# Two-layer hybrid decoder step: where the second expert choice of a half runs, and which engine adds expert rows that run alone

## The chip, the cores and the metric

The kernel is one launch on one NeuronCore of a Trainium2 chip. The metric is device time in microseconds (us) of one execution, input tensors and outputs in HBM. TensorE does matrix products, VectorE elementwise work, reductions and top-8 searches, ScalarE activations and copies, GpSimd issues the gathers, SyncE issues all other DMAs.

## The reference, cut to what matters

Two layers run over a prompt of 512 tokens (four tiles of 128) and over 8 sample tokens with caches. In each layer a token gets three mixers (a dilated window attention, a gated delta rule, a stick-breaking attention) and then PEER, a choice of 16 of 16384 one-neuron experts by each of 8 heads:

```python
s1, i1 = lax.top_k(s[:, :, 0], PEER_TOPK)
s2, i2 = lax.top_k(s[:, :, 1], PEER_TOPK)
top_s, pick = lax.top_k(cand_s, PEER_TOPK)            # 16 x 16 sums per head
act = jax.nn.gelu(jnp.einsum('nd,ned->ne', xk, u_tab[ik]))
return jnp.einsum('ne,ned->nd', gk * act, v_tab[ik])
```

So every token fetches 128 rows of 1024 floats from `peer_u`, takes a dot with each, and adds up 128 rows of `peer_v` with weights. The modulation vectors `silu(c) @ w_ada + b_ada` (6144 columns a layer) are needed by every normalisation.

## The kernel before, in words

The prompt is cut into halves of two tiles, and a half of one layer is a unit; there are four (layer 0 tiles 0, 1; layer 0 tiles 2, 3; layer 1 the same). The program is a row of windows, each an `nc.Block()` that all engines enter and leave together (`window`, line 2503). The first computes a part of layer 0's modulation. The second runs the mixers of unit 0 beside the mixers of the sample, with the modulation of layer 1 in it (`late`, line 2566). Then come four windows `k` = 0 to 3, each with the experts of unit `k` beside the mixers of unit `k + 1`; the last has the sample's second layer beside the experts of unit 3. In the profile the second window ends at 992 us, and the four expert windows begin at 993, 1937, 2785 and 3644 us.

The mixers of a unit are a list of stages (`token_mixers`, line 2276): normalise, `project` (14.7 MB of weights), unit lengths, heads, two attentions, delta rule in three stages, gated norm, `out_projection` (4 MB), normalise again, `queries` (4 MB), `choose_tile` for tile 0, `choose_tile` for tile 1. Each stage is a Python generator per engine, cut into ticks, and ends with a barrier (`stage_over`) of the lane's engines. `choose_tile` (line 1753) is VectorE work: `choose` (line 294) finds the 16 best by MAX8, FIND_INDEX8 and MATCH_REPLACE8 in 14 pieces; the last tick raises `chosen`.

The experts of a unit are a list of phases: all rows of `u` of tile a; rows of `v` of a and of `u` of b in turn; all rows of `v` of b. In what follows these are the `u` stretch (128 rows), the mixed stretch (256) and the `v` stretch (128, called alone, since its phase has one batch). A row is one gather of 128 partitions x 4 KB (512 KB) by GpSimd into one of GR = 12 buffers (line 2392); it waits for the buffer's last reader. A `u` row is one VectorE instruction (line 2442). A `v` row is either a product on TensorE with a diagonal matrix that ScalarE makes (lines 2479 and 2496; four matmul records of 512 columns) or one scalar_tensor_tensor on VectorE into ACC (line 2458). `on_dve` (line 168) gives VectorE every fourth row from row 8 on, 30 of 128. GpSimd waits for `chosen` before row 0 of each `u` batch.

What sets the order is a plan made ahead: every stage has a length (`paced`), `when` spreads the stages' ticks over 0 to 1 by these lengths, the expert rows are spread evenly over the same 0 to 1, and `merge` emits each engine's instructions in that one order. Nothing else than the order ties mixers to rows; each engine then runs its own stream in order. The lengths sum to 554 where the next unit has tiles 0, 1 (window k = 1) and to 606 where it has tiles 2, 3 (k = 0 and 2), each choice being 59 of it.

`modulate` (line 593) streams `w_ada` through a ring of SBUF tiles. SyncE's program for one tick: wait until a tile is used (613), load the next (614), wait for VectorE's result (618), store it (619), wait until the store has landed (620), load the next bias (621). Layer 1 is done in two stages of six tiles of 512 columns (2 MB) with a ring of two, one beside each choice of unit 0 (`meanwhile`).

SC[0] and SC[1] hold the scores of the two tiles. TMP, scratch of `project`'s convolution (lines 415 and 416), lies on SC[1].

## Time and profile before, and how to read it

| | us |
|---|---|
| median of 3 runs | 4719.75 (4712.13 to 4724.38) |
| the profiled execution, its own time | 4694.12 |
| its span, first to last instruction | 4692.3 |
| TensorE busy | 3425.7 (73%) |
| VectorE busy | 2843.8 (61%) |
| GpSimd busy | 2587.5 (55%) |
| mean granted TensorE clock | 0.843 |

A view of stretches gives, for each stretch of the span (us from its start), the busy time and instruction count of each engine, the granted clock as a share of full speed, the mean busy share of the 16 DMA engines, and GB/s. A view of waits gives the waiting engine, tile and line, what released it, then us in total, times, longest. A timeline row gives start, duration, engine, line, operation, count, and in brackets the idle time before it. A group row gives count, busy us, mean ns, and idle time before it with the releasers.

### The profile page before, as it was taken

To read this page: it belongs to the slowest core of one execution; us is meant where nothing else is said; L and a number is where in the kernel's file an instruction comes from. 1 tells how busy PE (TensorE), PEld (TensorE's weight loads), DVE (VectorE), ACT (ScalarE), POOL (GpSimd) and SP (SyncE) were. 2 spreads that over 40 slices of the span, in tenths; PEclk is the share of its full clock that TensorE was granted. 3 is DMA by queue.
4 is the path that set the end of the run, shared out by engine and by line. 5 is a ranking of instruction groups with operands and counts; after the bars stand their busy time and mean duration, and the time that the engine had idled before them with its cause. 6 is when DMAs were issued, how large, how long until landed. Compare 5 with 4: busy or idle time off the path is not lost. (4 is left out here: it accounts for less than half of the span.)

```text
span 4692.3 us, 42307 instructions
## 1 busy us (share of the span) xinstructions
PE 3425.7 (73%) x11982; PEld 1910.2 (41%) x11982; DVE 2843.8 (61%) x5777; ACT 877.2 (19%) x2045; POOL 2587.5 (55%) x2244
## 2 busy tenths in 40 slices
PE   5966768539298889575887967498898436748897
PEld 2624543126154554262455426255553113213351
DVE  1225552556866648787774688868649767584322
ACT  1113110011142112112321211242221011000120
POOL 0000362025767757687774667777656767665563
PEclk8986789759589999796998988799999767869896
DMA  6451375549989989899998889999988989999995
GB/s 229 139 180 56 101 227 177 187 104 320 354 318 345 385 308 339 331 399 342 366 376 320 306 334 395 353 346 361 367 306 308 378 303 348 362 382 377 336 330 154
DMA packets 586674, 1401.71 MB, mean 299 GB/s; under 512 B 67314, under 2 KB 287659, under 8 KB 585244
## 3 DMA queue, kind: packets, MB, share of 16 engines
q0 software_dynamic: 306176, 1107.44, 63.6%
q1 hardware_dynamic: 261836, 274.77, 17.7%
q10 hardware_dynamic: 18432, 16.79, 1.1%
q8 instruction: 101, 1.65, 0.1%
q14 instruction: 129, 1.06, 0.1%
HBM read 1387.11 MB, written 11.88 MB: 298 GB/s over the span
## 5 line engine op out<-in xcount | busy, mean ns | idle before, releaser
L2496 PE MATMUL bank<-arena 128*128 128x512 f32 (+1 forms) x3264 | 1589.6, 636 | 200.5 <-PEq L2493 117.9
L2392 POOL DMA_INDIRECT arena<-in_peer_u_dram,arena x1056 | 1279.6, 1212 | 693.2 <-issue 303.1
L2392 POOL DMA_INDIRECT arena<-in_peer_v_dram,arena x1056 | 1160.5, 1099 | 749.2 <-PE bank L2496 448.4
L2442 DVE CUSTOM_DVE_ANT_0 arena<-arena 128x1024 f32<-128x1024 f32 (+1 forms) x1056 | 1269.8, 1224 | 447.5 <-DMA arena<-in_peer_u_dram,arena 417.4
L2496 PEld LDWEIGHTS bank<-arena 128*128 128x128 f32 (+1 forms) x3264 | 614.8, 196 | 1013.6 <-issue 869.5
L2479 ACT ACTIVATE arena<-arena 128x128 f32<-128x128 f32 (+1 forms) x816 | 301.5, 394 | 1072.9 <-PE bank L2496 686.1
L2458 DVE SCALAR_TENSOR_TENSOR arena<-arena 128x1024 f32<-128x1024 f32 x232 | 297.6, 1283 | 243.6 <-DMA arena<-in_peer_v_dram,arena 223.3
L799 PE MATMUL bank<-arena 128*128 128x256 f32 (+3 forms) x1472 | 368.9, 414 | 101.0 <-PEq L792 95.9
L2138 POOL DMA_INDIRECT arena<-in_cache_sb_k_dram,arena x64 | 84.0, 1312 | 550.4 <-POOLq L2131 530.2
L799 PEld LDWEIGHTS bank<-arena 128*128 128x128 f32 (+1 forms) x1472 | 247.0, 170 | 220.8 <-issue 156.1
L641 PE MATMUL bank<-arena 128*9 128x512 f32 x384 | 180.3, 627 | 66.9 <-PEq L637 45.9
L796 PE MATMUL bank<-arena 128*128 128x256 f32 x768 | 177.7, 392 | 18.6 <-PEq L792 18.6
L1565 PE MATMUL bank<-arena 128*128 128x256 f32 (+1 forms) x640 | 154.0, 399 | 40.6 <-PEq L1563 39.0
L796 PEld LDWEIGHTS bank<-arena 128*128 128x128 f32 x768 | 149.1, 196 | 48.5 <-issue 27.7
L718 PE MATMUL bank<-arena 128*128 128x128 f32 (+1 forms) x160 | 31.5, 360 | 178.6 <-PEq L714 178.6
L1565 PEld LDWEIGHTS bank<-arena 128*128 128x128 f32 (+1 forms) x640 | 113.1, 178 | 87.9 <-issue 62.3
L655 DVE TENSOR_TENSOR arena<-bank,arena 9x512 f32<-9x512 f32 x24 | 16.3, 679 | 194.9 <-DVEq L654 194.9
L2167 PE MATMUL bank<-arena 128*4 128x256 f32 x512 | 118.2, 386 | 17.2 <-PEq L2116 15.7
L1647 PE MATMUL bank<-arena 128*128 128x256 f32 x512 | 117.7, 385 | 4.7 <-PEq L1643 3.7
L641 PEld LDWEIGHTS bank<-arena 128*9 128x9 f32 x384 | 35.0, 94 | 203.7 <-issue 203.1
L1647 PEld LDWEIGHTS bank<-arena 128*128 128x128 f32 x512 | 97.9, 193 | 30.2 <-issue 17.8
L718 PEld LDWEIGHTS bank<-arena 128*128 128x128 f32 (+1 forms) x160 | 26.3, 204 | 192.1 <-issue 192.0
(339 smaller groups left out, 3730.0 us busy)
## 6 DMA issues: line engine op xcount, KB each, us to landing
arena<-in_w_in_dram SPq DMA_DIRECT2D x78, 1024.0 KB, 13.2
arena<-in_w_ada_dram SPq DMA_DIRECT2D x24, 2048.0 KB, 8.4
arena<-in_w_out_dram SPq DMA_DIRECT2D x24, 1024.0 KB, 13.0
arena<-in_peer_wq_dram SPq DMA_DIRECT2D x24, 1024.0 KB, 15.0
arena<-in_peer_u_dram,arena POOLq DMA_INDIRECT x1056, 7.4
arena<-in_peer_v_dram,arena POOLq DMA_INDIRECT x1056, 6.2
arena<-in_cache_sb_k_dram SPq DMA_DIRECT2D x128, 128.0 KB
arena<-in_cache_sb_v_dram SPq DMA_DIRECT2D x128, 128.0 KB
```

What stands on the lines that cost most here:

```text
L641: last = pe_.matmul(ps[n % 2][0:R9, 0:width], CT[:, k, :], W[n % ring][:, k, :], start=(k == 0), stop=(k == KD - 1))
L796: last = pe_.matmul(ps[t % BANKS][:, 0:n_], m.W[c % ring][:, k, off:off + P], m.HT[:, k, 0:n_], start=(k == 0), stop=(k == KD - 1))
L799: last = pe_.matmul(ps[t % BANKS][0:r, 0:hi - lo], m.HT[:, k, i * P:i * P + r], m.W[c % ring][:, k, 0:hi - lo], start=(k == 0), stop=(k == ...
L1565: last = pe_.matmul(bank(g)[0:r, 0:CW_], m.OT[:, k, i * P:i * P + r], m.W[j % ring][:, k, 0:CW_], start=(k == 0), stop=(k == KD - 1))
L1647: last = pe_.matmul(ps[h % 3][:, 0:n_], m.W[h // 2 % ring][:, k, (h % 2) * P:(h % 2 + 1) * P], m.HT[:, k, 0:n_], start=(k == 0), stop=(k = ...
L2138: pool_.indirect_dma_start(m.HALF[h % 4][:, j, :], None, rows, bass.IndirectOffsetOnAxis(ap=m.IDP[:, at:at + 1], axis=0)).then_inc(paged[h ...
L2167: last = pe_.matmul(ps[b % 2][0:NH, 0:AW], weights[:, half * HP + j, :], m.HALF[n % 4][:, j, :], start=(half == 0 and j == 0), stop=(half ...
L2392: pool_.indirect_dma_start(G_[g % GR][0:b.parts, :], None, tables[0 if which == "u" else 1], bass.IndirectOffsetOnAxis(ap=b.index[:, n:n + ...
L2442: vec.tensor_tensor_reduce(row, row, b.h, 1.0, 0.0, ALU.mult, ALU.add, b.AV[0:b.parts, n:n + 1]).then_inc(freed_by_dve, 1)
L2458: i_ = vec.scalar_tensor_tensor(ACC, G_[g % GR], b.AV[:, n:n + 1], ACC, ALU.mult, ALU.add)
L2479: act_.activation(DG[order % NDG][0:b.parts, 0:b.rows], b.mark, ACT.Copy, scale=b.AV[0:b.parts, mine:mine + 1]).then_inc(diag_ready, 1)
L2496: last = pe_.matmul(ps[6 + i][0:b.rows, :], DG[owners[g][1] % NDG][0:b.parts, 0:b.rows], G_[g % GR][0:b.parts, i * GBLK:(i + 1) * GBLK], s ...
```

## The change

The second choice of a unit leaves the list of stages and becomes a thread of its own in the next window, spread over the first 0.22 of its plan, with a lane's set of semaphores of its own. The modulation of layer 1 becomes one stage of 24 tiles of 256 columns (1 MB) with a ring of four, beside unit 0's first choice, and that stage gets length 80. The sums of lengths become 495 and 547 (516 in the second window). Where a phase holds one batch, VectorE gets every second `v` row from row 8 on (60 of 128). TMP gets room of its own, since SC[1] is now in use during `project`.

```diff
+ON_DVE_ALONE = 2
-    return not b.sample and n >= FIRST_ON_DVE and n % ON_DVE == ON_DVE - 1
+    return not b.sample and n >= FIRST_ON_DVE and n % b.every == b.every - 1
...
-            m.CWR = AR.room(P)[0:KW * CC, :]
             m.SMALL = AR.room(16)
-            scratch = SC[1].rearrange("p a b -> p (a b)")
-            m.TMP = [scratch[:, i * n_:(i + 1) * n_] for i in range(3)]
+            m.TMP = [AR.room(n_) for _ in range(3)]
+            m.CWR = m.TMP[2][0:KW * CC, 0:P]
...
-                        paced(choose_tile(u, e, 0, meanwhile[0:1]), 59), paced(choose_tile(u, e, 1, meanwhile[1:2]), 59)]
+                        paced(choose_tile(u, e, 0, meanwhile), 80 if meanwhile else 59)]
...
+            for phase in phases:
+                for which, b in phase:
+                    if which == "v":
+                        b.every = ON_DVE_ALONE if len(phase) == 1 else ON_DVE
...
+        def second_choice(u, span):
+            ticks, programs = LC.choose_tile(u, None, 1)
+            return [span[0] + (span[1] - span[0]) * (n + 1) / ticks for n in range(ticks)], programs
...
+            times += [(t, 3, "choice") for t in choice[0]]
...
-                      experts=programs.get(name, nothing)())
+                      experts=programs.get(name, nothing)(), choice=choice[1].get(name, no_choice)())
...
-        LP, LS = lane("prompt", ps[0:6]), lane("sample", ps[6:8])
+        LP, LS, LC = lane("prompt", ps[0:6]), lane("sample", ps[6:8]), lane("second_choice", [])
...
-        tiles = [AR.room(KD, GBLK) for _ in range(2)]
-        late = [LP.modulate(1, tiles, GBLK, half * MOD // 2, (half + 1) * MOD // 2) for half in range(2)]
+        late = [LP.modulate(1, [AR.room(KD, GBLK // 2) for _ in range(4)], GBLK // 2)]
...
+            choice = second_choice(u, (0.0, 0.22))
             if k < 3:
-                window(LP.token_mixers(units[k + 1]), [], phases)
+                window(LP.token_mixers(units[k + 1]), [], phases, choice=choice)
...
-                window([], LS.token_mixers(samples[1], (LAST_at, arena_cols)), phases + [[("u", s)], [("v", s)]], (0.0, 0.85))
+                window([], LS.token_mixers(samples[1], (LAST_at, arena_cols)), phases + [[("u", s)], [("v", s)]], (0.0, 0.85), choice)
```

## Rows read from the trace of the kernel before

**Rows 1.** Stretches: columns PE, PEld, DVE, ACT, POOL busy, PE clock, DMA share, GB/s.

```profile
1067.00:1296.00 229.00, 124.26 (x481) 89.49 (x479) 181.43 (x321) 28.63 (x82) 160.32 (x128) 0.75 0.94 343
...
1937.00:2146.00 209.00, 117.94 (x481) 97.49 (x481) 167.34 (x293) 27.10 (x71) 168.94 (x128) 0.76 1.00 385
2146.00:2562.00 416.00, 319.80 (x1234) 195.24 (x1234) 285.85 (x494) 109.34 (x257) 284.21 (x257) 0.88 0.95 356
2562.00:2785.00 223.00, 204.72 (x565) 97.12 (x563) 159.34 (x508) 47.15 (x118) 139.45 (x129) 0.99 0.86 309
2785.00:3000.00 215.00, 119.72 (x482) 98.70 (x482) 177.76 (x312) 30.98 (x78) 165.56 (x128) 0.75 1.01 388
...
3402.00:3644.00 242.00, 215.11 (x602) 107.21 (x600) 158.83 (x508) 48.76 (x122) 135.77 (x129) 0.96 0.83 298
3644.00:3882.00 238.00, 95.97 (x338) 45.30 (x338) 152.44 (x268) 20.11 (x42) 170.99 (x128) 0.65 0.92 348
...
4365.00:4590.00 225.00, 203.59 (x619) 97.37 (x620) 61.31 (x97) 47.51 (x120) 128.45 (x128) 0.95 0.92 336
```

**Rows 2.** Stretches inside the `v` stretch of window 1: `queries`, first choice.

```profile
2562.00:2618.00 56.00, 55.44 (x232) 35.10 (x231) 12.30 (x14) 15.22 (x38) 27.67 (x27) 1.00 0.80 274
2618.00:2700.00 82.00, 77.43 (x179) 32.99 (x177) 71.68 (x245) 17.87 (x45) 57.75 (x53) 1.00 0.92 328
```

**Rows 3.** Timelines: ScalarE's last score copy of unit 0, VectorE's last instruction of that window.

```profile
747.67 2.05 ACT L1683 COPY arena<-bank 128x512 f32<-128x512 f32 x4 [3.48 <-ACTq L1680]
...
991.47 0.17 DVE L373 TENSOR_TENSOR arena<-arena 64x16 f32<-64x16 f32 x1
```

**Rows 4.** Timeline of SyncE's queue, 756 to 946 us: tiles of `w_ada`, last stores.

```profile
756.22 1.02 SPq L614 DMA_DIRECT2D arena<-in_w_ada_dram  x2
...
775.32 0.39 SPq L614 DMA_DIRECT2D arena<-in_w_ada_dram  x1
...
910.12 0.39 SPq L614 DMA_DIRECT2D arena<-in_w_ada_dram  x1
...
918.89 0.39 SPq L614 DMA_DIRECT2D arena<-in_w_ada_dram  x1
...
937.34 9.12 SPq L628 DMA_DIRECT2D modulation<-arena  x2
```

**Rows 5.** Waits of SyncE's queue, 749 to 967 us.

```profile
SPq L620 <- SPq L620: 55.2, 8, 7.7
```

**Rows 6.** DMA issues (KB each, us to landing), 88 to 156 and 770 to 812 us.

```profile
arena<-in_w_in_dram SPq DMA_DIRECT2D x12, 1024.0 KB, 5.2
...
arena<-in_w_ada_dram SPq DMA_DIRECT2D x4, 2048.0 KB, 8.2
```

**Rows 7.** VectorE's rows of choice and expert rows, 2618 to 2786 us: timelines and group.

```profile
2622.46 0.68 DVE L304 MAX8 arena<-arena 128x8 f32<-128x128 f32 x3 [5.42 <-SPq L2272]
...
2777.14 0.29 DVE L373 TENSOR_TENSOR arena<-arena 128x128 f32<-128x128 f32 x1
...
L2458 DVE SCALAR_TENSOR_TENSOR arena<-arena 128x1024 f32<-128x1024 f32 x26 | 33.4, 1284 | 6.9 <-DMA arena<-in_peer_v_dram,arena 3.8 <-DVEq L374 0.2
```

**Rows 8.** VectorE's waits for rows in `u` stretches 0 to 3, in order.

```profile
DVE arena L2442 <- DMA arena<-in_peer_u_dram,arena: 13.4, 16, 2.0
...
DVE arena L2442 <- DMA arena<-in_peer_u_dram,arena: 28.1, 26, 10.0
...
DVE arena L2442 <- DMA arena<-in_peer_u_dram,arena: 19.8, 21, 9.5
...
DVE arena L2442 <- DMA arena<-in_peer_u_dram,arena: 40.9, 73, 9.2
```

**Rows 9.** Page, part 5: matmuls of `out_projection` (1565) and of `queries` (1647).

```profile
L1565 PE MATMUL bank<-arena 128*128 128x256 f32 (+1 forms) x640 | 154.0, 399 | 40.6 <-PEq L1563 39.0
...
L1647 PE MATMUL bank<-arena 128*128 128x256 f32 x512 | 117.7, 385 | 4.7 <-PEq L1643 3.7
```

**Rows 10.** Timeline of TensorE: four expert rows back to back, 2720 us.

```profile
2719.45 7.10 PE L2496 MATMUL bank<-arena 128*128 128x512 f32 x16
```

More of the change, by code:

```diff
@@ L2296, in token_mixers @@
                         paced(out_projection(u, e), 36), paced(again, 14), paced(queries(u, e), 40),
-                        paced(choose_tile(u, e, 0, meanwhile[0:1]), 59), paced(choose_tile(u, e, 1, meanwhile[1:2]), 59)]
+                        paced(choose_tile(u, e, 0, meanwhile), 80 if meanwhile else 59)]
             it = Room()
             it.modulate, it.token_mixers, it.walk, it.ps, it.walked = modulate, token_mixers, walk, ps, 0
+            it.choose_tile = choose_tile
             return it
@@ L2501, in experts, with window @@
             return steps, {"pool": pool, "sp": sp, "dve": dve, "act": act, "pe": pe}
-        def window(of_prompt, of_sample, phases, sample_span=(0.0, 1.0)):
+        def second_choice(u, span):
+            ticks, programs = LC.choose_tile(u, None, 1)
+            return [span[0] + (span[1] - span[0]) * (n + 1) / ticks for n in range(ticks)], programs
+        def window(of_prompt, of_sample, phases, sample_span=(0.0, 1.0), choice=([], {})):
             steps, programs = experts(phases) if phases else (0, {})
@@ L2514, in window @@
             nothing = lambda: iter([None] * steps)
+            no_choice = lambda: iter([None] * len(choice[0]))
             def run(name, eng):
                 merge(plan, prompt=LP.walk(of_prompt, counts[0], name, eng), sample=LS.walk(of_sample, counts[1], name, eng),
-                      experts=programs.get(name, nothing)())
+                      experts=programs.get(name, nothing)(), choice=choice[1].get(name, no_choice)())
             with nc.Block() as block:
```

## The prediction

> **What bounds the kernel now.** The stretches come first, because the busy shares of the whole span mix stages with different limits. In a `u` stretch the DMA engines are full: share 1.00 at 385 GB/s in window 1, 1.01 at 388 in window 2, with VectorE at 167 of 209 us and 178 of 215 [rows 1]. The `v` stretches are another matter: 309 and 298 GB/s, and TensorE busy 205 of 223 and 215 of 242 [rows 1]. Four expert rows take it 7.10 us back to back, 1.78 each [rows 10], so 98 rows are 174 us by themselves. Inside a `v` stretch, `queries` has TensorE at 55.4 of 56 us and VectorE almost idle, while the choice has TensorE at 77 of 82 and VectorE at 72 [rows 2]: both at once. The mixed stretch has TensorE at 320 of 416 and DMA at 0.95 [rows 1], bound now by the one and now by the other. The end of the second window is read from timelines: unit 0's scores are complete at 750 us, the window ends at 992 [rows 3]. What sets that stretch is SyncE's queue, which waits 55 us for stores to land before it loads a next bias [rows 5].
>
> **The end of the second window.** The change takes one choice out of it, and loads the same 25 MB in 24 tiles of 1 MB. A store is issued behind a tile's load, and the eight waits for stores last 6.9 us each in the mean [rows 5], about as long as a load takes to land; so a tile's turn is its landing time plus what SyncE does around it. For 2 MB that is 8.2 us of landing [rows 6] in a turn of 8.8 (910.12 to 918.89) [rows 4]. A load of 1 MB in the same column shape lands in 5.2 [rows 6], so a turn should be near 6.0. A ring of four holds the same 4 MB as the two tiles before, whose fill took 19 us (756.22 to 775.32) [rows 4]; then 20 turns of 6.0 are 120, the last products and stores about 20 (two stores alone 9 [rows 4]), and the sample's query weights in the same queue some 6: 165 us. VectorE's choice, 60 us (below), lies beside it. The new lengths also move this stage from 0.787 to 0.845 of the plan, so a bit more of the sample's lane must be over before it begins. The window took 694 us for 0.787 (from 56 to 750), which would make 51 us of 0.058 if all of it came on top, and 0 if it filled gaps; I take 30, as both lanes share TensorE. With the 7 us from 750 to the first load at 756 [rows 3, 4], 30 + 7 + 165 = 202 after 750 us in place of 242: **−40**. Bounds by a turn of 5.2 and of 8.2: −56 and +4.
>
> **The choice in the `u` stretch.** Two choices in window 1 last from 2622.5 to 2777.4 with 26 expert rows of 1.3 us between their pieces [rows 7]: (155 − 34) / 2 = 60 us of VectorE each. Each of the four windows gets one choice, in its first 0.22, that is within the `u` stretch; in window 0 the 32 sample rows in front take 5 of the 17 pieces, so 44 remain. What hides it is the time in which VectorE waits for rows: 13, 28, 20 and 41 us [rows 8]. Exposed are 31 + 32 + 40 + 19 = 122. VectorE idles in these stretches for other reasons too: span less busy less row waits is 35, 14, 17 and 45 [rows 1, 8]. It runs in order, and such a wait shrinks only by as much as VectorE now comes late; I take a third, 37. That is **+85**, with bounds +11 (all of it) and +122 (none). What is late next is the row buffers: GpSimd stops 12 rows ahead, and the DMA engines that were full are no longer. The choice's exponential on ScalarE is one small instruction and costs nothing here, ScalarE being busy 31 of 215 us [rows 1]. The third thread's `chosen` comes before the last `u` rows of tile a are issued, so GpSimd should not wait for it; in window 3 it comes at step 120 of 128, when GpSimd stands some four rows short: a few us, within the bounds.
>
> **The mixed stretch.** With the lengths at 495 (547) for 554 (606), all mixers slide later. In windows 0 and 2 two thirds of `out_projection` leave the mixed stretch, in window 1 a third of it and half of `queries`. By the page's groups one unit's `out_projection` is 154.0 x 128 / 640 = 31 us and `queries` 117.7 / 4 = 29 [rows 9]; so some 21 to 26 us of TensorE leave each, and a weight load of a few MB. TensorE being 77% busy and the DMA engines 95%, I take two thirds, 17 a window: **−52**. Bounds 0 and −78.
>
> **The `v` stretch.** Every second row on VectorE takes 30 rows of 1.78 from TensorE and gives VectorE 30 of 1.3, with one choice of 60 gone. Window 1: before the choice stand 67 rows, of which 8 + 29.5 on TensorE, 67 us, with `queries` 29, `out_projection` 9 and a backlog of 8 mixed rows, 14: 119. The choice then has 515 x 59 / 495 = 61 rows, half of them on VectorE: 60 + 30.5 x 1.3 = 100. Here **VectorE is the bound**, at 1.64 us a row, where the two choices before ran 515 x 118 / 554 = 110 rows in 155, 1.41. With 8 for the end the stretch is 227 against 223 [rows 1]. Window 2 the same way: 40 rows, 71, with 29, 20 and 14, is 134; the choice with 55 rows 96; 238 against 242 [rows 1]. Window 0 is laid out as 2. I take **0** for the three, ±10 each. Window 3 has no prompt mixers: TensorE, 204 of 225 us [rows 1], loses 53, and the DMA engines become the bound, 336 GB/s x 225 us = 75.6 MB at 385 in 196: **−29** (bounds 0 and −53). ScalarE's 120 fewer diagonals lie beside TensorE and cost or save nothing. A row on VectorE beside the gathers has one cost to bound: a gather took 57.75 / 53 = 1.09 us where VectorE was 87% busy [rows 2] and 128.45 / 128 = 1.00 where it was 27% [rows 1]; 0 to 0.1 us a row, and as GpSimd has slack I take 0.
>
> On this the Trainium skill speaks against the change (SBUF — State Buffer, section Who interferes with whom): a VectorE instruction with two SBUF inputs contends with a GpSimd instruction that reads SBUF. The added rows have two, and were each to hold GpSimd for its 1.28 us, the 120 would make +154 and the sum +118; the rows just named show a tenth of a microsecond.
>
> TMP's new place costs nothing: addresses alone, and VectorE's and SyncE's work on it is as before.
>
> **Sum.** −40 + 85 − 52 + 0 − 29 = −36. Against the profiled execution's 4694.12 that is 4658; that execution is 25.6 us under the median of the runs, 4719.75, so the forecast in the median is **4684**, −0.8%. Faster or slower can be told from no change by about 0.3%, 14 us.
>
> **The rivals.**
> *VectorE binds the `u` stretches (slower).* No other idle time takes the choice (+37), and as VectorE leaves the stretch late it carries that into the mixed stretch, where the rows of tile b are its own, so the gain there goes (+52): +53, **4773**. For it: VectorE would be asked for 227 us in window 1's 209. Against: it has idle time in every mixed stretch, 130 us in window 1 [rows 1]. It decides where VectorE passes some 97% in the `u` stretches.
> *The tile chain takes the second window's gain (no change).* If a 1 MB turn costs what a 2 MB turn does, 20 x 2.2 = +44, **4728**. For it: the store waits. Against: 5.2 us [rows 6].
> *The choice finds room (more).* All idle time is used, +11 in place of +85: −110, **4610**. For it: windows 0 and 3, where the other idle is largest.
> *Rows on VectorE slow the gathers.* 0.1 us on each of the 512 rows that run alone, +51: **4735**. That is the mechanism of the skill's rule above, at the size that the rows bear out.
>
> **How the numbers follow.** Forecast 0.46, VectorE bound 0.21, more 0.14, tile chain 0.13, gathers 0.06. The likeliest's own range is 4654 to 4716, by the half widths of its terms. 4610 to 4785 leaves out half of the best and the worst part of the slower case, under 2 in 10. Faster: 0.37 of the forecast's own, the 0.14, and 0.01 of the chain's: 0.52. Same: the rest of the forecast's and most of the chain's, 0.19. Slower: 0.29.
>
> **What would show it.** In the changed profile: the second window over near 950 us with w_ada turns of 6 us (a turn of 8 is the chain rival); `u` stretches 15 to 35 us longer with VectorE above 90% and DMA below 370 GB/s; `v` stretches of windows 0 to 2 as long as before with TensorE below 80%, that of window 3 near 196; 352 scalar_tensor_tensor rows in place of 232, and 480 fewer matmul records for expert rows on TensorE. The forecast is wrong where the `u` stretches don't grow, or grow by 60, or the second window ends past 985.

## The result, and the profile after

The changed kernel took 4774.44 us (median of four runs, 4770.19 to 4788.49), beside 4715.94 for the kernel before (four runs, 4705.72 to 4724.38): a ratio on record of 1.0143, interval 1.0119 to 1.0166 (the two medians by themselves give 1.0124). It is slower by 58 us in the medians. The forecast was 4684, faster by 0.8%; the time lies inside the range of 4610 to 4785 but on its other side, close to the number of the rival in which VectorE binds (4773), and only in half for that rival's reason: the `u` stretches grew nearly as it said, and the rest of the loss lies elsewhere, as the stretches show.

The profiled execution took 4771.5 us; its span is 4769.7. The page's busy times (columns: engine, us, share, instructions) and its group of expert rows added by VectorE come first.

```profile
PE 3292.4 (69%) x11694; PEld 1857.3 (39%) x11694; DVE 2987.9 (63%) x5913; ACT 823.2 (17%) x1927; POOL 2651.2 (56%) x2244
...
L2463 DVE SCALAR_TENSOR_TENSOR arena<-arena 128x1024 f32<-128x1024 f32 x352 | 452.0, 1284 | 253.2 <-DMA arena<-in_peer_v_dram,arena 213.6
```

352 rows instead of 232 are on VectorE, and TensorE has 133 us less to do than before: the exchange took place. The next view is that of the stretches (columns as [rows 1]): `u`, mixed, `v` of windows 0 to 2, then the three of window 3.

```profile
1049.00:1315.00 266.00, 136.88 (x484) 97.70 (x482) 216.94 (x449) 28.74 (x81) 172.66 (x129) 0.73 0.87 297
1315.00:1687.00 372.00, 315.28 (x1238) 186.31 (x1239) 264.61 (x451) 112.85 (x246) 285.07 (x256) 0.92 0.98 366
1687.00:1949.00 262.00, 196.01 (x600) 105.97 (x598) 156.20 (x330) 42.25 (x103) 139.14 (x129) 0.92 0.83 296
1949.00:2200.00 251.00, 118.77 (x469) 98.19 (x469) 224.06 (x533) 23.84 (x69) 173.80 (x128) 0.74 0.91 325
2200.00:2574.00 374.00, 294.37 (x1094) 171.18 (x1092) 264.61 (x457) 102.05 (x245) 283.12 (x257) 0.88 0.98 370
2574.00:2825.00 251.00, 199.58 (x596) 105.86 (x596) 158.49 (x333) 42.12 (x103) 146.40 (x129) 0.92 0.85 310
2825.00:3074.00 249.00, 122.27 (x477) 100.26 (x477) 219.78 (x527) 27.37 (x71) 169.03 (x128) 0.73 0.91 324
3074.00:3467.00 393.00, 322.87 (x1225) 187.34 (x1225) 279.15 (x473) 121.43 (x266) 288.06 (x258) 0.88 0.95 353
3467.00:3736.00 269.00, 206.07 (x624) 112.81 (x624) 155.94 (x330) 42.47 (x103) 144.59 (x129) 0.89 0.82 291
3736.00:3975.00 239.00, 96.61 (x341) 46.13 (x341) 201.68 (x501) 21.48 (x42) 182.62 (x129) 0.64 0.95 349
3975.00:4453.00 478.00, 318.45 (x800) 120.03 (x801) 326.29 (x457) 49.59 (x127) 318.55 (x256) 0.83 0.99 369
4453.00:4670.00 217.00, 169.31 (x523) 77.95 (x522) 98.68 (x126) 35.25 (x92) 134.96 (x128) 0.91 0.95 350
```

The same boundaries (first gather of one stretch to first gather of the next) give the table for all that follows; the predicted change stands beside the measured one.

| us | before | after | change, windows 0, 1, 2, 3 | sum | predicted |
|---|---|---|---|---|---|
| end of the second window | 993 | 978 | | −15 | −40 |
| sample's rows in front of window 0 | 74 | 71 | | −3 | – |
| `u` stretches | 230, 209, 215, 239 | 266, 251, 249, 239 | +36, +42, +34, 0 | +112 | +85 |
| mixed stretches | 411, 416, 401, 482 | 372, 374, 393, 478 | −39, −42, −8, −4 | −93 | −52 |
| `v` stretches | 230, 223, 242, 226 | 262, 251, 269, 217 | +32, +28, +27, −9 | +78 | −29 |
| after the last row | 101 | 99 | | −2 | – |

The column sums to +77, the difference of the two spans (4769.7 − 4692.3); the medians are only 58 apart, as the profiled execution of before lies under its median. Two readings. In the `u` stretches VectorE went from 167 to 224 us in window 1 and the DMA engines from 385 GB/s down to 325: VectorE, at 89% of the stretch, now sets its pace (`e4` below, without the second choice, shows that). In the `v` stretches of windows 0 to 2 neither TensorE (75 to 80%) nor VectorE (58 to 63%) nor DMA (291 to 310 GB/s) is full over the whole stretch; it must be split to be read. The two rows for window 1 answer to [rows 2]: what stands ahead of the choice, and the choice.

```profile
2574.00:2723.00 149.00, 136.89 (x485) 84.59 (x485) 64.05 (x69) 32.53 (x80) 85.82 (x77) 0.94 0.90 330
2723.00:2816.00 93.00, 62.69 (x112) 21.27 (x112) 88.13 (x259) 8.44 (x22) 60.14 (x52) 0.91 0.85 305
```

In the first part TensorE is busy 137 of 149 us and VectorE 64; in the second VectorE 88 of 93 and TensorE 63. The stretch is bound by two engines one after the other, and each stands partly idle while the other binds. Rows are counted here by their gathers, which run ahead of a row's use by up to 12 buffers. By that count 77 rows were issued in the first part and 51 in the second; before, 30 in the first (60 us, 2.0 each) and 98 beside the two choices (155 us, 1.58 each). A row now costs 1.9 us in the first part and 1.8 in the second: the rows moved to the dear part, and those that stayed beside a choice became dearer too.

### The profile page after: what moved, and what is told of

The parts are those of the page before. It is cut to its first block and busy times, and to the rows that moved or that the text cites. A ratio compares the mean times of both kernels' runs of the same rounds, so it can differ in the third digit from the quotient of the medians.

```text
span 4769.7 us, 41908 instructions
## 1 busy us (share of the span) xinstructions
PE 3292.4 (69%) x11694; PEld 1857.3 (39%) x11694; DVE 2987.9 (63%) x5913; ACT 823.2 (17%) x1927; POOL 2651.2 (56%) x2244
## 5 line engine op out<-in xcount | busy, mean ns | idle before, releaser
L2397 POOL DMA_INDIRECT arena<-in_peer_u_dram,arena x1056 | 1300.8, 1232 | 763.4 <-issue 293.3
L2501 PE MATMUL bank<-arena 128*128 128x512 f32 (+1 forms) x2784 | 1434.9, 657 | 297.9 <-DMA arena<-in_peer_v_dram,arena 171.1
L2397 POOL DMA_INDIRECT arena<-in_peer_v_dram,arena x1056 | 1201.2, 1137 | 695.7 <-PE bank L2501 386.1
L2501 PEld LDWEIGHTS bank<-arena 128*128 128x128 f32 (+1 forms) x2784 | 526.5, 201 | 1038.1 <-issue 731.3
L2463 DVE SCALAR_TENSOR_TENSOR arena<-arena 128x1024 f32<-128x1024 f32 x352 | 452.0, 1284 | 253.2 <-DMA arena<-in_peer_v_dram,arena 213.6
L799 PE MATMUL bank<-arena 128*128 128x256 f32 (+3 forms) x1472 | 389.7, 429 | 133.6 <-PEq L792 128.5
L2484 ACT ACTIVATE arena<-arena 128x128 f32<-128x128 f32 (+1 forms) x696 | 248.8, 393 | 869.9 <-PE bank L2501 438.3
L799 PEld LDWEIGHTS bank<-arena 128*128 128x128 f32 (+1 forms) x1472 | 259.7, 180 | 262.6 <-issue 192.7
L641 PE MATMUL bank<-arena 128*9 128x256 f32 (+1 forms) x576 | 182.2, 475 | 48.2 <-PEq L637 31.2
L796 PE MATMUL bank<-arena 128*128 128x256 f32 x768 | 181.8, 397 | 26.5 <-PEq L792 26.5
L796 PEld LDWEIGHTS bank<-arena 128*128 128x128 f32 x768 | 151.0, 199 | 58.3 <-issue 37.0
L899 PE MATMUL bank<-arena 128*128 128x256 f32 x64 | 28.1, 587 | 185.3 <-PEq L897 185.3
L1565 PEld LDWEIGHTS bank<-arena 128*128 128x128 f32 (+1 forms) x640 | 111.9, 176 | 62.8 <-issue 34.4
L1647 PE MATMUL bank<-arena 128*128 128x256 f32 x512 | 115.7, 380 | 0.0
## 6 DMA issues: line engine op xcount, KB each, us to landing
arena<-in_w_in_dram SPq DMA_DIRECT2D x78, 1024.0 KB, 10.2
```

Source lines behind the costliest of these rows:

```text
L641: last = pe_.matmul(ps[n % 2][0:R9, 0:width], CT[:, k, :], W[n % ring][:, k, :], start=(k == 0), stop=(k == KD - 1))
L796: last = pe_.matmul(ps[t % BANKS][:, 0:n_], m.W[c % ring][:, k, off:off + P], m.HT[:, k, 0:n_], start=(k == 0), stop=(k == KD - 1))
L799: last = pe_.matmul(ps[t % BANKS][0:r, 0:hi - lo], m.HT[:, k, i * P:i * P + r], m.W[c % ring][:, k, 0:hi - lo], start=(k == 0), stop=(k == ...
L1565: last = pe_.matmul(bank(g)[0:r, 0:CW_], m.OT[:, k, i * P:i * P + r], m.W[j % ring][:, k, 0:CW_], start=(k == 0), stop=(k == KD - 1))
L1647: last = pe_.matmul(ps[h % 3][:, 0:n_], m.W[h // 2 % ring][:, k, (h % 2) * P:(h % 2 + 1) * P], m.HT[:, k, 0:n_], start=(k == 0), stop=(k = ...
L2397: pool_.indirect_dma_start(G_[g % GR][0:b.parts, :], None, tables[0 if which == "u" else 1], bass.IndirectOffsetOnAxis(ap=b.index[:, n:n + ...
```

## The experiments

Eleven kernels ran. Times below are medians; ratios stand against the kernel before on the same chip (4705.69 in the first group of four, 4709.15 in the second, 4710.45 in the third), and are those on record, which differ from the quotient of two medians by up to 0.1%.

**One row in four on VectorE everywhere (`e1_alone_every4`).** The changed kernel without its third part.

```diff
-ON_DVE_ALONE = 2
+ON_DVE_ALONE = 4
```

> The changed kernel with one part undone: rows that run alone go to VectorE one in four, as before. Theory 1 (the choice in the u stretch is the price; the slide of the mixers moves time from the mixed to the v stretches at about no gain; every second row gives little): v stretches of windows 0 to 2 within 15 us of the changed kernel's 262, 251, 269, that of window 3 longer by 5 to 15, total 4775 to 4810. Theory 2 (rows on VectorE are the price, since they stand behind the mixers' waits in VectorE's order): v stretches shorter by 20 or more each, total 4720 or less.

4779.82 us, ratio 1.0149 (1.0128 to 1.0171). The `v` stretches of windows 0 to 2 are 256, 252, 273, as good as unchanged, and only that of window 3 is longer, by 19, a little more than the 5 to 15 expected. So the added rows are not the price. The same two parts of window 1's `v` stretch:

```profile
2581.00:2749.00 168.00, 158.43 (x536) 94.12 (x536) 43.54 (x53) 37.92 (x92) 82.48 (x78) 0.96 0.82 296
2749.00:2825.00 76.00, 75.09 (x175) 33.08 (x175) 71.28 (x244) 15.24 (x39) 56.82 (x51) 1.00 0.98 366
```

With fewer rows on VectorE the choice is shorter by 17 us, and what stands ahead of it longer by 19: the rows trade TensorE's time ahead of the choice for VectorE's time in it, and nothing is left over.

**The added rows alone (`e2_before_every2`).** The kernel before with every second row on VectorE where a phase has one batch.

```diff
-    return not b.sample and n >= FIRST_ON_DVE and n % ON_DVE == ON_DVE - 1
+    return not b.sample and n >= FIRST_ON_DVE and n % b.every == b.every - 1
...
+                        b.every = ON_DVE_ALONE if len(phase) == 1 else ON_DVE
```

> The kernel before with that part alone: every second row that runs alone on VectorE, both choices still at the end. By VectorE's load the two choices with 55 rows beside them take 120 + 72 = 192 us where they took 155, queries gets 5 to 10 us shorter, window 3's v stretch 10 to 30 us shorter: theory 1 gives 4750 to 4790 (slower than before by 35 to 75). Theory 2 gives over 4800. If the rows are a gain wherever they stand, 4690 or less.

4762.19 us, 1.0124 (1.0103 to 1.0144). The two choices of window 1 together now run 183 us in place of 155 (192 were expected), with VectorE at 95% and TensorE at 66%:

```profile
2634.00:2817.00 183.00, 120.75 (x216) 41.14 (x214) 173.06 (x513) 20.02 (x52) 118.46 (x100) 0.90 0.82 293
```

The `v` stretches of windows 0 to 2 grew by 22, 25 and 20; that of window 3, which has no choice, shrank by 16. So here a second row on VectorE gains only where TensorE alone binds.

**The choice that stays, at the length of the two that were there (`e3_old_lengths`, `e5_choice_length_90`).** The choice of a half's first tile gets length 118 or 90 in the plan in place of 59 (windows 0 to 2); the rest is the changed kernel.

```diff
-                        paced(choose_tile(u, e, 0, meanwhile), 80 if meanwhile else 59)]
+                        paced(choose_tile(u, e, 0, meanwhile), 80 if meanwhile else 118)]
```

> The changed kernel with the plan's lengths as they were: the first choice gets length 118, so that all mixers stand at the rows where they stood before, and the choice is spread over 100 to 110 rows. Theory 1: u stretches within 10 us of the changed kernel's 266, 251, 249, mixed stretches back to 410, 416, 402, v stretches back to 230 or below; total 4750 to 4800. Theory 3 (out_projection at the switch to the v stretch is the price): total 4735 or less.

> The changed kernel with length 90 for the remaining choice (the change has 59, the run before it 118): the choice stands beside 88 rows in window 1 and 80 in windows 0 and 2, about where VectorE's load (60 + 0.65 us a row) meets a row pace of 1.36 us. Theory 4 (the slide costs because the choice is squeezed onto 55 to 61 rows, where VectorE binds at 1.64 us a row): total 4715 to 4740, as with 118 or a little below; the choice itself 110 to 120 us in the trace. Theory 3 (out_projection at the switch to the v stretch): the same total, since with this length out_projection ends at the switch; so this run only shows whether the loss is gone between 59 and 90.

At 118: 4735.0 us, 1.0055 (1.0033 to 1.0077). The mixed stretches are back at 412, 411 and 398, the `v` stretches at 214, 207 and 215, so of the changed kernel's +78 in the `v` stretches and −93 in the mixed ones both are gone, and these six stretches sum to 1857 us where the changed kernel has 1921. The total is 15 us under the lowest that was expected on this reading, and at the bound given for a rival, that `out_projection` at the switch to the `v` stretch is the price; `e6` is for that. At 90: 4704.74, 0.9986 (0.9968 to 1.0003), 70 us under the changed kernel, by one number of the plan, and level with the kernel before; 4715 to 4740 had been expected. Window 1 at length 118, ahead of the choice and in it, and the same two parts at 90:

```profile
2606.00:2663.00 57.00, 56.18 (x232) 35.09 (x231) 17.99 (x19) 14.91 (x38) 33.01 (x30) 1.00 0.82 280
2663.00:2795.00 132.00, 97.88 (x195) 34.13 (x195) 114.34 (x279) 19.41 (x48) 103.35 (x95) 0.97 0.98 369
```

```profile
2580.00:2676.00 96.00, 88.52 (x330) 53.91 (x331) 37.06 (x38) 22.47 (x57) 51.94 (x52) 0.93 0.91 333
2676.00:2783.00 107.00, 79.38 (x162) 28.48 (x161) 101.66 (x267) 15.21 (x37) 83.82 (x76) 0.98 0.99 372
```

In the changed kernel 51 gathers were issued in the choice's 93 us; here 95 in 132, and 76 in 107 at length 90: 1.4 us a row in place of 1.8, and the DMA engines are full beside it (0.98 and 0.99). A row moved into the choice costs little there: from 51 to 76 rows the choice grows by 14 us (93 to 107), or 0.6 a row, about half of VectorE's 1.28 us for one row in two. What it costs ahead of the choice is read in `e6`. The length decides how many rows share the choice's time, and 59 gave it too few.

**Where the mixers stand in the plan (`e6_switch_after_out_projection`).** A rival to the last reading: the cost is not in the number of rows beside the choice, but in that `out_projection` slid into the `v` stretch. Length is moved from `delta_inverse` to `queries`, so that `out_projection` stands in the mixed stretch again, with the choice at 59.

```diff
-                        paced(delta_inverse(u, m), 64), paced(delta_scan(u, m), 18), paced(gated_norm(u, e, first_w_out), 9),
-                        paced(out_projection(u, e), 36), paced(again, 14), paced(queries(u, e), 40),
+                        paced(delta_inverse(u, m), 64 if meanwhile else 34), paced(delta_scan(u, m), 18), paced(gated_norm(u, e, first_w_out), 9),
+                        paced(out_projection(u, e), 36), paced(again, 14), paced(queries(u, e), 40 if meanwhile else 70),
```

> The changed kernel with 30 of length taken from delta_inverse and given to queries in windows 0 to 2: out_projection then ends ahead of the v stretch, while the choice keeps its 59. Theory 3: mixed and v stretches of windows 0 to 2 together shorter by 40 to 75, total 4700 to 4735. Theory 4: together within 20 of the changed kernel's, total 4755 to 4795, choices still 95 to 103 us each.

4785.35 us, 1.016 (1.0124 to 1.0195). The mixed stretches went to 421, 403 and 426, the `v` stretches to 225, 235 and 233: together 646, 638 and 659, against 634, 625 and 662 in the changed kernel. Moving the stage moves time from one stretch to the other and saves none; the choices still took 92, 93 and 89 us for 48, 51 and 44 rows (95 to 103 us were expected). So the place of `out_projection` by itself is not the price, as far as this way of moving it shows. Window 1, ahead of the choice and in it:

```profile
2609.00:2742.00 133.00, 112.31 (x372) 61.89 (x370) 50.59 (x47) 25.43 (x68) 83.26 (x77) 0.94 0.94 340
2742.00:2835.00 93.00, 58.26 (x110) 20.58 (x111) 87.68 (x258) 9.40 (x22) 59.99 (x52) 0.93 0.85 307
```

`out_projection` stands in neither these parts nor those of `e5`, so the two runs can be set side by side: with 25 rows fewer ahead of the choice, `e5` is shorter there by 37 us (133 to 96), 1.5 a row, and longer by 14 in the choice. In windows 0 and 2 the part ahead is shorter by 21 and 27 us for 25 and 24 rows.

**The second choice left out (`e4_no_second_choice`).** The tile's lists and weights are copied from the other tile's in the last tick.

```diff
-            ticks, programs = LC.choose_tile(u, None, 1)
+            ticks = CHOOSE_YIELDS + 3
...
+                        vec.tensor_copy(IDI[u.sets + 1], IDI[u.sets]).then_inc(dve_own, 1)
...
+                        vec.tensor_copy(GT[u.sets + 1], GT[u.sets]).then_inc(dve_own, 1)
...
+                        vec.sem_inc(chosen, 1)
...
+            programs = {"dve": dve}
```

> The changed kernel without the second choice: tile b takes tile a's lists (two copies on VectorE), all else in its place; the choice of 256 of the 512 prompt rows a layer is left out. Theory 1: u stretches back to 230, 212, 215 or a bit less, mixed and v stretches as in the changed kernel: total 4640 to 4690. Theories 2 and 3: 4735 or more.

4648.76 us, 0.9882 (0.9856 to 0.9908), 126 under the changed kernel. The `u` stretches of windows 0 to 2:

```profile
1047.00:1275.00 228.00, 131.63 (x491) 93.72 (x489) 175.33 (x310) 27.38 (x79) 163.44 (x131) 0.77 0.95 346
1930.00:2142.00 212.00, 118.18 (x473) 97.15 (x473) 177.14 (x310) 20.84 (x61) 173.29 (x128) 0.77 0.99 382
2755.00:2961.00 206.00, 113.63 (x478) 94.03 (x478) 168.99 (x297) 27.13 (x71) 166.99 (x128) 0.78 1.01 391
```

They are back where they were: by the boundaries of the table 225, 212 and 206 in place of 266, 251 and 249, and in windows 1 and 2 DMA is full again; that of window 3 is 239 to 240 with the choice or without. So the choice costs 39 to 43 us in each of windows 0 to 2 and nothing in window 3: all of what the `u` stretches grew is the choice's, and these three account for 123 of the 126 us.

**The choice in half the span (`e10_choice_in_011`).** Is it VectorE's load as a sum, or that its pieces hold up rows where they stand? The pieces are put twice as close.

```diff
-            choice = second_choice(u, (0.0, 0.22))
+            choice = second_choice(u, (0.0, 0.11))
```

> The changed kernel with the second choice within the first 0.11 of the plan in place of 0.22. If its price in the u stretch is VectorE's load as a sum (theory 1): u stretches 255 to 275, 240 to 260, 240 to 260, total 4760 to 4795. If the price comes from the pieces standing in front of rows, which are twice as dense here and pass what 12 buffers cover: u stretches longer by 15 to 30 each, total over 4810. If VectorE would have had time later in the stretch: shorter, below 4750.

4772.17 us, 1.0126 (1.0082 to 1.0171); the `u` stretches 247, 254 and 259 (266, 251, 249 in the changed kernel). The sum is within 6 us of what it was, but window 0 is to be left out of it: with the denser pieces more than half of its choice falls beside the sample's rows, ahead of the `u` stretch (VectorE is busy 58 us there in place of 39), and so the stretch is shorter by 19. Windows 1 and 2 hold all pieces in their `u` stretch either way, and there +3 and +10 us stand against the 15 to 30 that pieces in front of rows were expected to cost. So the price is in the main the load; up to 10 us may be the placing.

**`modulate` in tiles of 2 MB (`e8_modulation_512`).** The changed kernel with 12 tiles of 512 columns and a ring of two.

```diff
-        late = [LP.modulate(1, [AR.room(KD, GBLK // 2) for _ in range(4)], GBLK // 2)]
+        late = [LP.modulate(1, [AR.room(KD, GBLK) for _ in range(2)], GBLK)]
```

> The changed kernel with the modulation of layer 1 in one stage of 12 tiles of 512 columns and a ring of two. If SyncE's turns set the end of the second window (24 of 6 to 7 us against 12 of 9 to 10), that window ends 25 to 45 us earlier than the changed kernel's 977 us and the total is 4730 to 4750. If what precedes the stage or the sample's lane sets it, the end moves by under 10 us: 4765 to 4785.

4780.1 us, 1.0154 (1.0122 to 1.0186). The second window ended at 989, 11 us later than the changed kernel's: neither the 25 to 45 us earlier nor the change of under 10 that were expected. Its loads and last stores on SyncE's timeline:

```profile
809.46 3.11 SPq L614 DMA_DIRECT2D arena<-in_w_ada_dram  x2
...
830.75 0.39 SPq L614 DMA_DIRECT2D arena<-in_w_ada_dram  x1
...
940.24 0.39 SPq L614 DMA_DIRECT2D arena<-in_w_ada_dram  x1
...
970.16 0.65 SPq L628 DMA_DIRECT2D modulation<-arena  x2
```

The ten loads from 830.75 to 940.24 are 12.2 us apart in the mean, with the sample lane's loads between some of them in the same queue; the kernel before had turns of 10.3 to 8.4, the 8.8 of [rows 4] among them. From the first load to the last stores it is 161 us here and 166 in the changed kernel, so the size of the tiles moved that by 5 us alone. The other terms of the 11 us are a start that is 7 later and a tail that is 9 longer: between 971 and 987 VectorE runs the end of the prompt's and of the sample's choice, pieces of which stand between the products of `modulate` in its order. So SyncE's turns don't set the end alone. Why the start is later stays open.

**Versions built on the finding (`e7_last_unit_only`, `e9_rows_before_choice`, `e11_unit3_rows_every4`).** `e7` is the kernel before with three things: only unit 3's second choice goes to the next window (window 3, where it costs nothing); the first choice of unit 3 keeps length 118; every second row is VectorE's in windows 2 and 3 only.

```diff
+                second = [] if u.choice_later else [paced(choose_tile(u, e, 1, meanwhile[1:2]), 59)]
...
+                        paced(choose_tile(u, e, 0, meanwhile[0:1]), 118 if u.choice_later else 59)] + second
...
+                        b.every = ON_DVE_ALONE if len(phase) == 1 and b.late_unit else ON_DVE
...
+            u.choice_later = k == 3
...
+            b.late_unit = k >= 2
```

> The kernel before with the change only where the runs so far showed it free: unit 3's second choice alone moves into window 3, unit 3's first choice gets length 118, and every second row that runs alone goes to VectorE in windows 2 and 3 alone; the modulation and the other choices as before. Theory 1 with what the runs showed (the choice costs 40 us in the u stretches of windows 0 to 2 and nothing in window 3's, where VectorE waits for rows and for the sample's lane): window 2's v stretch 242 to 215, window 3's u stretch 236 to 245, its v stretch 226 to 212, total 4650 to 4680. If the choice costs 40 in window 3 too: 4690 to 4720.

4672.52 us, 0.9929 (0.9903 to 0.9954): faster than both kernels. The `v` stretch of window 2 is 216 (242 before), the `u` stretch of window 3 239 as before, its `v` stretch 220 (226). Window 2's `v` stretch, ahead of the choice and in it:

```profile
3414.00:3494.00 80.00, 74.39 (x292) 46.99 (x292) 24.68 (x26) 18.52 (x48) 42.02 (x41) 0.98 0.85 311
3494.00:3611.00 117.00, 83.92 (x173) 29.28 (x172) 106.88 (x272) 17.11 (x42) 91.88 (x83) 1.00 0.98 368
```

`e11` is `e7` with one row in four everywhere, and so asks which of `e7`'s parts brings it.

```diff
-ON_DVE_ALONE = 2
+ON_DVE_ALONE = 4
```

> The run with the change for unit 3 alone, with one row in four on VectorE everywhere. It parts the move of the choice from the rows. By TensorE's load (0.75 x 1.78 = 1.34 us a row beside the choice, VectorE at 60 + 100 x 0.25 x 1.3 = 93 us): window 2's v stretch 225 to 235 (216 with every second row, 242 before), window 3's 225 (220 with every second row), total 4685 to 4700. If the move alone gives all of it: 4665 to 4680.

4680.5 us, 0.9948 (0.9922 to 0.9974). The two intervals overlap, so the medians don't part the two; the traces do in part: the `v` stretches are 227 and 230 with one row in four, 216 and 220 with one in two. So the move of the choice gives 15 of the 26 us in window 2's `v` stretch (242 to 227), the rows 11. The choice there takes 117 us in both, with the DMA engines at 0.98 in both, whether TensorE is full (`e11`) or VectorE stands at 91% (`e7`); the part ahead of it takes 90 in place of 80:

```profile
3399.00:3489.00 90.00, 80.64 (x305) 49.89 (x306) 17.18 (x21) 19.92 (x51) 38.12 (x39) 0.96 0.78 274
3489.00:3606.00 117.00, 116.52 (x268) 50.17 (x268) 80.93 (x253) 27.75 (x68) 91.42 (x84) 1.00 0.98 369
```

So the rows belong on VectorE ahead of the choice. `e9` follows that: `e7`, and in windows 0 and 1 every second one of rows 8 to 27 too, those that stand ahead of the two choices.

```diff
+    every = ON_DVE_ALONE if b.alone and n < 28 else b.every
+    return not b.sample and n >= FIRST_ON_DVE and n % every == every - 1
...
+                        b.alone = len(phase) == 1
```

> The run with the change for unit 3 alone, and in windows 0 and 1 every second of the rows 8 to 27 of the v stretch on VectorE too, which come before the choices; the rows beside the choices stay one in four. By TensorE's load in queries (1.78 us a row): 5 to 10 us off the v stretch of windows 0 and 1, total 10 to 20 below the run for unit 3 alone (4672), 4650 to 4668. If rows on VectorE cost where the mixers wait: no change or longer.

4649.3 us, 0.9876 (0.9842 to 0.991), 1.2% under the kernel before and the fastest that was run with the whole computation. The part ahead of the choices takes 63 us in window 0 and 55 in window 1, 69 and 60 before; the two choices stayed at 154 and 156. These 11 us are what the edit shows; the rest of the 23 between the medians of `e9` and `e7`, which come from two chips, was not traced.

```profile
1699.00:1762.00 63.00, 59.84 (x248) 37.89 (x246) 20.15 (x21) 14.90 (x38) 33.84 (x32) 1.00 0.84 310
2554.00:2609.00 55.00, 54.24 (x227) 34.07 (x225) 17.18 (x19) 13.74 (x35) 31.34 (x29) 1.00 0.83 285
```

## Why the prediction was wrong, by its own steps

The sum said −36 and the spans differ by +77: 113 us were missed. By the table, 50 of these lie in the mixed and `v` stretches of windows 0 to 2 (−52 and 0 predicted, −89 and +87 measured), 27 in the `u` stretches, 25 in the second window, 16 in window 3's mixed and `v` stretches (−29 against −4 and −9); the other rows of the table make −5.

**The `v` stretch of windows 0 to 2: the step that failed.** It said 0, by two parts. The part on the choice held nearly: 100 and 96 us predicted for windows 1 and 2, 93 and 89 measured, with VectorE at 95% of it. The part on what stands ahead of the choice did not: 119 us predicted and 149 measured in window 1, 134 and 171 in window 2. TensorE's groups of that part, first of window 1, then of window 2 (count, busy us, mean ns, then idle time before it):

```profile
L2501 PE MATMUL bank<-arena 128*128 128x512 f32 x173 | 81.4, 616 | 4.1 <-PEq L2498 4.0
L1647 PE MATMUL bank<-arena 128*128 128x256 f32 x128 | 28.9, 379 | 0.0
L1565 PE MATMUL bank<-arena 128*128 128x256 f32 x96 | 23.8, 409 | 5.2 <-PEq L1563 5.2
...
L2501 PE MATMUL bank<-arena 128*128 128x512 f32 x175 | 85.0, 627 | 10.2 <-PEq L2498 7.6 <-DMA arena<-in_peer_v_dram,arena 2.6
L1565 PE MATMUL bank<-arena 128*128 128x256 f32 x128 | 30.2, 391 | 0.0
...
L718 PE MATMUL bank<-arena 128*128 128x128 f32 x16 | 3.4, 388 | 4.3 <-PEq L714 4.3
L1638 PE MATMUL bank<-arena 128*128 128x128 f32 x8 | 1.9, 424 | 9.8 <-PEq L1636 9.8
```

The expert rows are as reckoned: 81.4 and 85.0 us, where 67 + 14 and 71 + 14 stood in the sum, and `queries` 28.9 in window 1 as its 29. Three terms are not. `out_projection` took 23.8 and 30.2 in place of 9 and 20: more of it had slid past the boundary than the lengths said. The scores, norms and transposes around it (lines 1659, 718, 1638) were not counted, 8 to 9 us. And TensorE stood idle for 12 of the 149 and 24 of the 171 us, waiting at the ends of short stages (PEq, lines 714, 1563, 1636, 2498): the sum had it busy throughout, as `queries` alone in [rows 2] had shown it, 55.4 of 56. The granted clock there was 0.94 and 0.92, where [rows 2] has 1.00.

The deeper fault is that the step took the rows of each part from the new lengths and compared a row's cost only within the choice (1.64 us against 1.41, on 110 rows by the plan where the trace counts 98 gathers), not with a row's cost ahead of it. Before, 98 rows ran beside two choices at 1.6 us; now 51 run beside one at 1.8 and 77 ahead of it, where TensorE has rows and mixers both and each row comes to 1.9, as the 30 there did before at 2.0. With length 90, and nothing else altered, the mixed and `v` stretches of windows 0 to 2 sum to 1851 us (408, 388, 395, 221, 217, 222), 72 less than the 1923 of the kernel before and 70 less than the 1921 of the changed kernel: the gain of 52 that was forecast is there, and the length of the remaining choice takes it away. `e3` and `e5` show this, and `e6` shows that the place of `out_projection` alone does not bring it.

**The mixed stretch: more than its bound, and not a gain by itself.** −52 with a lower bound of −78 was predicted, −93 measured, of which −89 in windows 0 to 2. The mixers took more than their TensorE time with them, and it came back in the `v` stretches; in `e3`, with the old sum of lengths, both changes are gone.

**Window 3's `v` stretch**, predicted at −29, came to −9: DMA moved 350 GB/s in it and not the 385 that were assumed. One row in four there costs 19 us (`e1`) and one in two in the kernel before gives 16 (`e2`), so the direction was right; the size was half to two thirds of the 29 in those two runs and a third in the changed kernel.

**The `u` stretch: right in kind, mis-sized.** +85 was predicted and +112 measured; without the choice it is gone (`e4`). One term was too large: 60 us is how long a choice lasts in [rows 7] less its expert rows, and part of that is idle time of VectorE. The choice's own instructions (lines 305 to 374) sum to 55 us of VectorE in each of windows 1 to 3, and to 40 in the `u` stretch of window 0. The cover was too large by more. The step took the row waits of [rows 8] and a third of the other idle time as cover, in all four windows alike. VectorE's waits for rows in `u` stretches 0 to 3 of the changed kernel, and GpSimd's waits for VectorE in 1:

```profile
DVE arena L2447 <- DMA arena<-in_peer_u_dram,arena: 30.8, 12, 17.1
...
DVE arena L2447 <- DMA arena<-in_peer_u_dram,arena: 16.4, 15, 10.1
...
DVE arena L2447 <- DMA arena<-in_peer_u_dram,arena: 20.0, 10, 9.2
...
DVE arena L2447 <- DMA arena<-in_peer_u_dram,arena: 10.7, 4, 9.6
```

```profile
POOL arena L2397 <- DVE arena L2447: 44.3, 20, 5.1
```

Of the 13, 28, 20 and 41 us that were to be used up, 31, 16, 20 and 11 are there now. In each window the longest, of 9 to 17 us, stands at the stretch's start and is not filled. What is late next is as the step said, the row buffers: GpSimd now waits 44 us for VectorE in window 1. Against the stretches without the choice (`e4`), windows 0 to 2 exposed 41, 39 and 43 us of its 40, 55 and 55, nearly all; window 3, whose 41 us were in 73 waits, most of them short, hid all of its 55, where 19 less a share was predicted as exposed. VectorE's idle time of every kind, span less busy in the rows of stretches, went from 48, 42, 37 and 86 us to 49, 27, 29 and 37. The sum had 25, 33, 26 and 56 of it used, by one rule for all four; −1, 15, 8 and 48 were.

**The end of the second window: the chain right, its start late, and a tail left out.** The 165 us from the first load to the last stores were 166 (802.66 to 969.1). ScalarE's last score copy of unit 0, TensorE's timeline before it, and SyncE's queue after it:

```profile
800.38 2.05 ACT L1683 COPY arena<-bank 128x512 f32<-128x512 f32 x4 [0.56 <-ACTq L1680]
```

```profile
768.85 3.72 PE L1647 MATMUL bank<-arena 128*128 128x256 f32 x16
772.50 3.62 PE L2167 MATMUL bank<-arena 128*4 128x256 f32 x16
776.04 10.63 PE L1647 MATMUL bank<-arena 128*128 128x256 f32 x48
```

```profile
802.66 9.74 SPq L614 DMA_DIRECT2D arena<-in_w_ada_dram  x4
818.51 0.39 SPq L614 DMA_DIRECT2D arena<-in_w_ada_dram  x1
...
953.16 0.39 SPq L614 DMA_DIRECT2D arena<-in_w_ada_dram  x1
965.87 3.23 SPq L628 DMA_DIRECT2D modulation<-arena  x2
```

The scores are complete at 802.4, where they were at 749.7 [rows 3]: 53 us later and not 30, about the 51 given as the case in which all that is slid comes on top. The trace agrees with that case: TensorE goes from unit 0's `queries` (line 1647) to the sample's products (line 2167) and back with no idle time, so what the sample's lane does earlier, unit 0 does later. The gap of 6 us from the scores to the first load is gone. The turns were 7.1 us in the mean ((953.16 − 818.51) / 19, the sample's loads among them), not 6.0, and the fill and the end took less.

The reading of the kernel before was wrong in a part that the sum didn't show. SyncE's queue can't be all that sets that stretch: it loads no tile between 805 us and 877.69, where the second of the two stages begins, and its last stores are issued by 946.5 [rows 4]. In the 47 us from there to the first gather VectorE runs the rest of the prompt's choice and the sample's.

```profile
877.69 5.83 SPq L614 DMA_DIRECT2D arena<-in_w_ada_dram  x2
```

So the −15 is made of three terms: the first load 46.4 us later (756.2 to 802.7), the way from it to the last stores 23.8 shorter (190.2 to 166.4), and the tail behind them 37.7 shorter (47.0 to 9.3). The prediction ended with the last stores and had no tail; its −40 missed the later start, 16 us, and those 9. What sets the end is only partly shown; it isn't the turns alone (`e8`).

**The rivals.** The slower one gave 4773, but it had the gain of the mixed stretch gone and the `v` stretches at their forecast; its first half alone, +122 in the `u` stretches with no other idle time used, was near the measured +112. The gathers that VectorE might slow were no cause of this size. The Trainium skill (SBUF — State Buffer, section Who interferes with whom) has a VectorE instruction with two SBUF inputs contend with a GpSimd instruction that reads SBUF. In the choice of window 1, with VectorE at 95%, a gather took 60.14 / 52 = 1.16 us, against 1.09 at 87% [rows 2]; but in `e5`, at 95% too, it took 83.82 / 76 = 1.10, and in `e11`, at 69%, 91.42 / 84 = 1.09. The added rows on VectorE took 1284 ns each, as those before did [rows 7]. So what a gather takes doesn't follow VectorE's share, and no run here shows the contention.

**The signs that were named.** The forecast was to be wrong where the `u` stretches don't grow, or grow by 60, or the second window ends past 985. In windows 0 to 2 they grew by 34 to 42, only in window 3 not at all, and the second window ended at 978: these signs were not set on the step that failed. Of the signs in favour three failed: the second window's end near 950, the `v` stretches of windows 0 to 2 as long as before, and window 3's near 196 (217).

## What to carry to other kernels

Work that leaves a stretch takes the cover it gave to others with it: before moving a load off the engine that shares a stretch with a stream of rows, count how many rows run beside it under the new plan, and set its length so that both engines end together (here 60 us of choice, pauses between its pieces included, plus 0.65 us a row on VectorE, against the 1.4 us a row that the DMA engines allowed: 60 / 0.75, about 80 rows; length 90 gave 76 and beat 59 by 70 us). A stretch's idle time is not cover by its sum: here many short waits took up the moved work, and a long one at the stretch's start took up none. Before a queue is called the limit of a stretch, look for the time in which it issues nothing. And an engine is to be chosen for rows by which one binds in each part of a stretch, not in the stretch: one row in two on VectorE gained 5 to 19 us where TensorE bound and lost 20 to 25 where VectorE did.

## What the runs showed of the hardware that was not expected

VectorE at 95% of a stretch did not keep the DMA engines from 372 GB/s and share 0.99 beside it (`e5`'s choice of window 1): the same engine load with fewer rows to issue had left them at 305. The 24 tiles of 1 MB landed in 5.2 us, as the 1 MB loads of another tensor had done in a stretch without gathers [rows 6]; over the whole run of the changed kernel, gathers beside many of them, that tensor's took 10.2 in the median (page, part 6).

```profile
arena<-in_w_ada_dram SPq DMA_DIRECT2D x24, 1024.0 KB, 5.2
```
